# Products of constants on TensorE between the steps of four RMS norms

## The reference

```
first block:   h = rms_norm(x);  proj = h @ w_in
               y_a = (two RG-LRU scans of conv(proj_a)) @ p_a;  y_b = pooled branch @ p_b
               x = x + (gates_a*y_a + gates_b*y_b) @ w_out            (norm 2 reads this x)
               h = rms_norm(x);  up = conv(h @ w_up)
               x = x + (gelu(up_1)*up_2) @ w_down                     (norm "g", then norm 3)
               x = rms_norm(x)
second block:  u = rms_norm(x)*(1+scale1) + shift1;  S5 branch and sparse attention of u @ w_in_2
               x = x + gate1*(merged @ w_out_2)                       (norm 5 reads this x)
               u = rms_norm(x)*(1+scale2) + shift2
               x = x + gate2*((silu(u @ w_gate)*(u @ w_up)) @ w_down) (norm 6 reads this x)
               return rms_norm(x)

rms_norm(x) = x * rsqrt(mean(x*x over the 1024 channels) + 1e-6) * g
```

## Time and profile before

| | |
|---|---|
| median of 3 runs | 1651.01 us (1647.5 to 1651.02) |
| profiled execution, its own time | 1649.9 us |
| its span, first to last instruction | 1648.6 us |
| mean granted clock of TensorE | 0.976 |
| TensorE busy | 1572.1 us (95%), 6520 instructions |
| VectorE, ScalarE, GpSimd busy | 849.4, 864.2, 334.0 us |

### The profile page before, as it was taken

How to read it: one execution, slowest core, us unless ns; L and a number is a source line. 1 busy time by engine, 2 the same in 40 slices (tenths; PEclk the granted TensorE clock), 3 DMA queues, 4 the chain that set the end, 5 groups by cost and what they waited for, 6 DMA issues and landing times.

```text
span 1648.6 us, 17560 instructions
## 1 busy us (share of the span) xinstructions
PE 1572.1 (95%) x6520; PEld 1203.7 (73%) x6520; DVE 849.4 (52%) x1700; ACT 864.2 (52%) x1091; POOL 334.0 (20%) x348
## 2 busy tenths in 40 slices
PE   6899999999999999999999878989999999999997
PEld 5687888787788888888776545546687888888885
DVE  6778634464587765435349999863464122111011
ACT  5678768744554555434454415557545444444441
POOL 2111111111111111111133335542211111111111
PEclk9999999999999999999899989999998999999998
DMA  8677787899799898998587545419596998888872
GB/s 261 155 161 188 171 203 186 209 306 321 210 247 255 198 219 208 276 246 223 137 218 188 138 123 153 115 48 290 165 234 150 234 230 199 185 184 195 194 174 77
DMA packets 93893, 324.64 MB, mean 197 GB/s; under 512 B 10464, under 2 KB 10464, under 8 KB 93552
## 3 DMA queue, kind: packets, MB, share of 16 engines
q0 software_dynamic: 37856, 137.76, 44.9%
q1 hardware_dynamic: 52128, 178.28, 31.6%
q10 hardware_dynamic: 3824, 7.47, 1.2%
HBM read 177.59 MB, written 16.78 MB: 118 GB/s over the span
## 4 chain that ended last, share of the span: by engine, by line
PE 82%; DVE 10%; ACT 4%; issue 1%; DMA 1%; POOL 1%; ACTq 0%; DVEq 0%
PE ps L663 26%; PE ps L664 25%; PE ps L666 25%; PE ps L827 1%; DVE pl_f L1877 1%; DVE sml L1874 1%; DVE pl_f L1821 1%; PE ps L727 1%; PE ps L933 1%; PE ps L705 1%; PE ps L904 1%; DVE pl_f L1823 1%; ACT whi L1009 1%; ACT wlo L1016 1%; DVE pl_f L1482 1%
## 5 line engine op out<-in xcount | busy, mean ns | idle before, releaser
L663 PE MATMUL ps<-pl_r,whi 128*128 128x512 f32 x1976 | 795.5, 403 | 27.2 <-DVE pl_f L1817 11.7
L664 PE MATMUL ps<-pl_r,wlo 128*128 128x512 f32 x1976 | 785.8, 398 | 0.0
L666 PE MATMUL ps<-pl_r,whi 128*128 128x512 f32 x1976 | 785.1, 397 | 0.0
L663 PEld LDWEIGHTS ps<-pl_r,whi 128*128 128x128 f32 x1976 | 374.5, 190 | 143.7 <-issue 30.2
L666 PEld LDWEIGHTS ps<-pl_r,whi 128*128 128x128 f32 x1976 | 374.0, 189 | 92.0 <-DVE pl_r L1414 0.4
L664 PEld LDWEIGHTS ps<-pl_r,wlo 128*128 128x128 f32 x1976 | 374.6, 190 | 88.3 <-issue 0.3
L2020 POOL DMA_DIRECT2D wlo<-raw x246 | 213.1, 871 | 1103.2 <-ACT wlo L1016 1077.7
L1009 ACT ACTIVATE whi<-raw 128x1024 fp32r<-128x1024 f32 x247 | 259.9, 1052 | 178.8 <-PE ps L666 141.7
L1016 ACT ACTIVATE wlo<-raw 128x1024 fp32r<-128x1024 f32 x246 | 257.4, 1046 | 0.0
L1994 DVE TENSOR_TENSOR pl_f<-ps,pl_f 128x512 f32<-128x512 f32 x22 | 15.2, 692 | 179.0 <-PE ps L666 179.0
L1398 DVE TENSOR_TENSOR pl_r<-pl_f,pl_r 128x512 fp32r<-128x512 f32 x112 | 77.6, 693 | 36.9 <-ACT pl_r L1036 21.0
(11 more groups left out here) (229 smaller groups left out, 1333.3 us busy)
## 6 DMA issues: line engine op xcount, KB each, us to landing
wlo<-raw POOLq DMA_DIRECT2D x246, 512.0 KB, 6.2
raw<-in_w SPq DMA_DIRECT2D x245, 512.0 KB, 5.3
pl_f<-in_mod SPq DMA_DIRECT2D x48, 512.0 KB, 9.0
tab<-pl_f SPq DMA_DIRECT2D x16, 512.0 KB, 6.7
pl_f<-tab POOLq DMA_DIRECT2D x16, 512.0 KB, 4.2
spill<-pl_f ACTq DMA_DIRECT2D x16, 256.0 KB, 3.5
pl_f<-spill SPq DMA_DIRECT2D x16, 256.0 KB, 4.8
pl_f<-in_x SPq DMA_DIRECT2D x12, 256.0 KB, 8.3
```

The costliest lines, as they stand in the source:

```text
L663: matmul(out, wh, sr(pair, kk, "hi"), start=start, stop=False)
L664: matmul(out, wl, sr(pair, kk, "hi"), start=False, stop=False)
L666: mm = matmul(out, wh, sr(pair, kk, "lo"), start=False, stop=stop)
```

## The change

A helper `keep_warm(*widths)` is added to TensorE's list. It takes a bank, computes one fp32 product for each width, of the identity (stationary) with the first columns of `k.vec`, and gives the bank back. Nobody reads it. It is called in the three waits of norms 2, 3 and 5 and in the first two of norm 6: with 480 and 256 columns before the last sums, with 128 (256 in norm 3) between sums and rows, with 480 and 256 between rows and the next stage. Nothing else differs.

```
@@ -718,6 +719,16 @@
+    def keep_warm(*widths):
+
+        nonlocal warm
+        warm += 1
+        b = take("warm", warm)
+        for w in widths:
+            mm = matmul(b[:, 0:w], k.ident, k.vec[:, 0:w], start=True, stop=True)
+        mm.then_inc(*done.tick(None, ("warm", warm)))
+        give("warm", warm)
@@ norm 2; norm 5 is the same with sums([5], 7), to_rows(5) and FIRST_FFN_2 @@
+    keep_warm(480, 256)
     sums([2], 7)
+    keep_warm(128)
     to_rows(2)
+    keep_warm(480, 256)
     first(FIRST_UP, "h2")
@@ norm 3 @@
+    keep_warm(480, 256)
     sums([3, "g"], 7)
+    keep_warm(256)
     to_rows(3)
+    keep_warm(480, 256)
     first(FIRST_IN_2, "u")
     to_rows("g")
```

More of the change, by code:

```diff
@@ L640, in tensor_engine @@
     ready = set()
+    warm = 0
     k.plan.clear()
```

## The result

The changed kernel takes 1637.63 us (median of 4 runs, 1635.25 to 1641.82) against 1650.99 (1647.5 to 1651.02): ratio 0.9927, interval 0.990 to 0.9954. Two later comparisons of the same pair gave 0.9936 (0.9922 to 0.9949) and 0.9943 (0.9926 to 0.996). The three ratios stand for gains of 9.4 to 12.1 us; their intervals reach from 6.6 to 16.5. The forecast was 1641.6, range 1638.0 to 1646.5.

The account below looks back on a forecast made before the run. TensorE was taken as the bound, its clock halving in the norms' pauses. Gains of 2.1, 4.7, 3.4 and 0.75 us sum to 11.0, or 9.4 with norm 3's exception: 1649.9 - 9.4 + 1.1 = 1641.6 us, range 1638 to 1646.5.

Parts of the forecast that it names:

- Norm 2: Pauses before the next stage: full clock gives back 0.92 us in rows and 1.2 in first products, together 2.1.
- Norm 5: Full clock gives back 0.3 us in sums, 0.92 in rows and 2.2 in first products, together 3.4.
- Norm 6: At the kernel's end, eight more row products at full clock bring ScalarE's copy earlier, a gain of 0.75 us.
- Norm 3 with the clock held: Full clock gives back 1.65 us in sums, 0.92 in rows and 2.14 in first products, together 4.7.
- Norm 3's exception: Clock expected to fall once more after norm 3's sums despite the fills, so norm 3 gives 3.1 us.
- the last fill at half clock ... comes 0.7 late: Norm 3's third pause: a 2.56 us fill against about 1.7 plus 0.16 us of drain, ending 0.7 late.
- The price of 2.56 us: Time of a large fill (480 and 256 columns) at 1.2 GHz, against 1.28 us at full clock.
- That the fills cost nothing: At full clock every fill ends some 0.2 to 0.4 us before its wait does; without cover, 10.1 us at most.
- The widening by 2 us for the middle: Stage 921 to 1180 may shift with its own clock falls, so the range's low end went from 1640.0 to 1638.
- The rival of the late fills: Clock does not hold; third fills of norms 2, 3 and 5 end 2.66 us late in all: 1653.7 us, chance 0.09.
- The rival that nothing changes: The fall answers to something other than these pauses and the fills stay hidden: 1651.0 us, chance 0.06.
- The rival of some norms only: Clock holds in some norms only, half the sum, 5.5 us: 1645.5, between 1643.5 and 1648, chance 0.17.

Follow-up runs that it names:

- the two later looks: The kernel before, profiled two more times with no edit; 1648.13 and 1648.0 us.
- the second execution: The changed kernel run and profiled again with no edit; 1638.43 us, ratio 0.9936 to the kernel before.
- the third: The changed kernel run and profiled once more, unedited, beside the version with extra fills; 1638.93 us, ratio 0.9943 to the kernel before.
- the third-pause kernel: Changed kernel keeping only the fills between rows and the next stage (norms 2, 3, 5); 1644.31 us, ratio 0.9973.
- the kernels with one pause filled: Changed kernel with only the fills before the sums (1642.96 us, ratio 0.9959), or only those between rows and next stage (1644.31 us, 0.9973).
- second execution with more fills: Repeat of the changed kernel plus fills in norm 1 and the wait at 58 us, and two norm 3 edits; 1635.15 us, ratio 0.9922.

## Why the prediction was right, and where it was off

- **The mechanism** is shown: fills of the same number with one column each give nothing (ratio 1.0003), with their columns the clock stays at 1.00 and every norm shortens; and leaving out norm 3's fills changes norm 3 alone.
- **Norm 2**: predicted 2.1, measured 11.19 - 9.18 = 2.0. **Norm 5**: 3.4, measured 3.3. **Norm 6**: 0.75, measured 15.11 - 14.36 = 0.75. **Norm 3 with the clock held**: 4.7, measured 15.29 - 10.71 = 4.6. The sum 11.0 was 10.7. That is against the one profile of the kernel before that the prediction read; against the two later looks norm 2 gives up to 2.2, norm 3 4.4 to 4.5 and norm 6 0.9 to 1.1.
- **Norm 3's exception** was real in two of the changed kernel's three profiled executions and absent in one. Its rows' part, 0.92, was measured as 0.92. The mis-sized term is "the last fill at half clock ... comes 0.7 late": it came on time. I had the whole fill at half clock; in the second execution the clock was back about 0.8 us after the fill began (PEclk 0.50 in 796 to 797, 0.85 in the next microsecond), and in the third 0.5 us after. The price of 2.56 us itself was about right, 2.43 by the third-pause kernel. Norm 3 then gave 3.7, not 3.1. With that the sum is 9.7 to 10.7 us, against 9.4 forecast.
- **That the fills cost nothing** held: behind each the trace still has a wait for ScalarE or VectorE, of 0.21 to 0.52 us where the clock held; behind the 128-column one it lists none, yet the rows start at 413.68 because VectorE's reciprocal ended at 413.63.
- **The difference between the median and the profile** is outside the change. The profiled executions stand 10.1 us apart. The first of them came to norm 2's last product 0.72 us later than the kernel before and had the long middle. The median of 1637.63 lies nearer to executions with a short one: two of its four runs took 1635.25 and 1635.43. They were not profiled, so that this is their cause is not shown. The widening by 2 us for the middle was needed and slightly too small: the middle scatters by 4.3 us. Of the 2.6 us between the forecast of 1641.6 and the 1639.0 by the ratio, 0.3 to 1.3 are norm 3's; the rest is within this scatter.
- **The rival of the late fills** was cheaper than priced: by the second product 1.3 us late over three norms, not 2.66. What it left out is the earlier rise in return: from the first row product to the 13th product the three norms are 3.1 us shorter in all. **The rival that nothing changes** is refuted. **The rival of some norms only** describes the kernels with one pause filled.

## What to carry to other kernels

Where TensorE is the bound, look at the granted clock around every short stop: here stops of 0.5 to 1.75 us, three in a row, were enough for the clock to halve, which cost 2 to 5 us in norms 2, 3 and 5 and 0.75 us at the end, on top of the stops. Fill them with streams of columns that need nothing and end just before the wait does. One-column products did not do it, and a fill that delayed the first product by 0.4 to 0.5 us cost 0.2 to 0.45 us, less than the mildest fall (0.9). Work out such a gain by rows of the same operation at the two clock levels, and compare intervals between fixed instructions, not spans: the middle of this kernel alone scatters by 4 us.

## What the runs showed of the hardware

- Products of one column, although they keep TensorE listed as busy, did not hold the clock: with every fill cut to one column it fell in all four norms. Norm 3, with 1.84 us of one-column sums ahead of the first pause and 1.95 us behind, lost the clock in four of the seven executions with all fills in place, while norms 2 and 5 with half as many sums kept it in each. That the sums are what sets norm 3 apart is likely and not shown: its second pause is longer too (0.90 us against 0.48).
- The clock rose during products of constants (second execution of the changed kernel: 0.50 from 796 to 797, 0.85 in the next microsecond) and of ones (second execution with more fills: 0.50 from 19 to 20, 0.87 in the next). It held at 1.00 on float32 transposes in norms 2, 3 and 5.
- What low clock costs depends on what waits for TensorE: between norm 3 and 1010, 10 us more at 1.2 GHz went with at most 0.5 us of time, the 3.4 us near 1170 with 1.3 to 1.6.
- The fall came at very different distances from the last full product, also between executions of one kernel: with fills in the first pause only, norm 2 never lost the clock and norm 5 lost it after its rows.
